# Next slot's tokens turned behind unit 31 into free halves of PSUM, and turns of one part side by side, in the expert stage of an encoder

## The reference, cut to what matters

```python
logits = (h @ router)                        # 8 experts
top_v, top_i = lax.top_k(logits, 2)
top_w = softmax(top_v)                       # gates
y = sum_e gates[:, e] * ((silu(h @ w1[e]) * (h @ w3[e])) @ w2[e])
# h: 256x1024, w1, w3: 8x1024x3584, w2: 8x3584x1024, float32
```

## Time and profile before

| | us |
|---|---|
| median of three runs | 1703.61 (1702.89 to 1704.52) |
| the profiled execution | 1703.97 |
| its span in the trace | 1702.1 |
| expert stage in it | about 700 to 1690 |
| PE busy | 1632.4 |
| DVE busy | 1249.7 |
| ACT busy | 1046.9 |

### The profile page before, as it was taken

How to read it: one execution, slowest core, us unless ns; L and a number is a source line. 1 busy time by engine, 2 the same in 40 slices (tenths; PEclk the granted TensorE clock), 3 DMA queues, 4 the chain that set the end, 5 groups by cost and what they waited for, 6 DMA issues and landing times.

```text
span 1702.1 us, 22766 instructions
## 1 busy us (share of the span) xinstructions
PE 1632.4 (96%) x8953; PEld 1403.5 (82%) x8953; DVE 1249.7 (73%) x916; ACT 1046.9 (62%) x926; POOL 101.7 (6%) x92
## 2 busy tenths in 40 slices
PE   5999999999999999899999999999999999999996
PEld 5899989999888998688787787787887887887885
DVE  4655575454565556798788887888887987987995
ACT  4364645343535463776676776776776776776774
POOL 1000001000000000110000000000000000000540
PEclk8999999999999999999999999999999999999999
DMA  7544459554654447999999999999999999999970
GB/s 240 193 143 148 149 192 341 184 189 151 227 176 143 148 149 285 352 372 419 348 374 369 363 369 347 368 369 350 377 377 335 387 377 336 387 377 336 406 312 25
DMA packets 162477, 488.97 MB, mean 287 GB/s; under 512 B 8176, under 2 KB 12368, under 8 KB 162416
## 3 DMA queue, kind: packets, MB, share of 16 engines
q1 hardware_dynamic: 154576, 459.17, 73.7%
q0 software_dynamic: 7552, 27.89, 4.3%
q10 hardware_dynamic: 288, 1.05, 0.2%
HBM read 471.82 MB, written 16.25 MB: 287 GB/s over the span
## 4 chain that ended last, share of the span: by engine, by line
PE 89%; ACT 4%; DVE 3%; issue 2%; DMA 2%; SPq 0%; DVEq 0%; ACTq 0%
PE big L1558 21%; PE big L1560 21%; PE big L1559 21%; PE small L1558 6%; PE small L1560 6%; PE small L1559 6%; PE small L1603 2%; ACT ehi L958 2%; DMA raw<-ffn_w 1%; DMA raw<-w_in 1%; ACT whi L756 1%; DVE elo L1378 0%; DVE wlo L1049 0%; PE small L1718 0%; PE small L1658 0%
## 5 line engine op out<-in xcount | busy, mean ns | idle before, releaser
L1378 DVE TENSOR_TENSOR elo<-eraw,ehi 128x2048 fp32r<-128x2048 f32 x336 | 772.7, 2318 | 137.2 <-ACT ehi L958 136.1
L958 ACT ACTIVATE ehi<-eraw 128x2048 fp32r<-128x2048 f32 x336 | 642.1, 1918 | 280.2 <-PE small L1560 147.2
L1049 DVE TENSOR_TENSOR wlo<-raw,whi 128x2048 fp32r<-128x2048 f32 (+2 forms) x104 | 229.9, 2218 | 202.6 <-ACT whi L756 202.6
L756 ACT ACTIVATE whi<-raw 128x2048 fp32r<-128x2048 f32 (+2 forms) x104 | 192.5, 1860 | 263.6 <-PE big L1560 187.9
L1558 PE MATMUL big<-ehi,hehi 128*128 128x512 f32 x896 | 352.0, 393 | 1.4 <-DVE helo L1423 1.4
L1560 PE MATMUL big<-ehi,helo 128*128 128x512 f32 x896 | 349.1, 390 | 0.0
L1559 PE MATMUL big<-elo,hehi 128*128 128x512 f32 x896 | 348.8, 389 | 0.0
L1558 PE MATMUL big<-hhi,whi 128*128 128x256 f32 x864 | 248.4, 288 | 9.4 <-DVE hlo L1069 8.6
L1560 PE MATMUL big<-hhi,wlo 128*128 128x256 f32 x864 | 246.0, 285 | 0.0
L1559 PE MATMUL big<-hlo,whi 128*128 128x256 f32 x864 | 245.9, 285 | 0.0
L1558 PEld LDWEIGHTS big<-ehi,hehi 128*128 128x128 f32 x896 | 168.3, 188 | 36.3 <-DVE helo L1423 1.6
(11 more groups left out here) (326 smaller groups left out, 1766.4 us busy)
## 6 DMA issues: line engine op xcount, KB each, us to landing
eraw<-moe_w SPq DMA_DIRECT2D x336, 1024.0 KB, 5.4
raw<-ffn_w SPq DMA_DIRECT2D x30, 1024.0 KB, 5.0
raw<-w_gate SPq DMA_DIRECT2D x24, 1024.0 KB, 5.0
raw<-w_in SPq DMA_DIRECT2D x20, 1024.0 KB, 5.2
raw<-w_branch SPq DMA_DIRECT2D x12, 1024.0 KB, 4.9
raw<-w_o SPq DMA_DIRECT2D x8, 1024.0 KB, 5.0
xs_all<-zeros POOLq DMA_DIRECT2D x12, 512.0 KB, 8.4
xn<-xs_all POOLq DMA_DIRECT2D x8, 512.0 KB, 6.0
```

The source lines that it names most:

```text
L756: act.activation(whi[u % HI][:, 0:kt, 0:cols], raw[u % RAW][:, 0:kt, 0:cols], ACT.Copy).then_inc(hi_ready, 1)
L958: act.activation(ehi[HI_OF[n]][:, :], eraw[n % RING][:, :], ACT.Copy).then_inc(ehi_ready, 1)
L1049: dve.tensor_tensor(wlo[u % RAW][:, 0:kt, 0:cols], raw[u % RAW][:, 0:kt, 0:cols], whi[u % HI][:, 0:kt, 0:cols].bitcast(F32), ALU.subtract) ...
L1378: dve.tensor_tensor(elo[n % RING][:, :], eraw[n % RING][:, :], ehi[HI_OF[n]][:, :].bitcast(F32), ALU.subtract).then_inc(elo_ready, 1)
```

## The change

`TURNS` changes so that the two parts of one pair are turned behind the same unit (10, 19, 31 instead of 9 and 10, 18 and 19, 30 and 31). The places where ScalarE and VectorE take them are now in a table of their own, `TAKEN`. The last part, still turned behind unit 37, is taken at unit 40 instead of 41. The next slot's tokens are turned in one block of eight behind unit 31, into the second halves of `big[0]` and `big[1]`, which pair 3 doesn't use, and taken at units 39 and 40 as before; ScalarE waits there for unit 35, the last that reads the old tokens. The turns of the last part no longer wait for a `helo` copy but for the copies of part 5.

```diff
--- before.py
+++ after.py
@@ -76,8 +76,13 @@
 
 
 
-TURNS = [9, 10, 18, 19, 30, 31, 37]
-GATHERS = [35, 36]
+
+TURNS = [10, 10, 19, 19, 31, 31, 37]
+TAKEN = [14, 14, 23, 23, 35, 35, 40]
+
+
+GATHERED = 31
+HE_TAKEN = [39, 40]
 HE = 2 * PAIRS - 1
 RING, EHI, EHI_WORK = 14, 4, 3
 EARLY = 3
@@ -733,9 +738,9 @@
         MIX_LOADS = 5
         BLOCK_COLS = ((0, P), (P, TOKENS))
 
-        def gather_bank(i):
-
-            return 3 - i
+        def gather_place(s, i):
+
+            return small[:, 3 - i, :] if isinstance(s, int) and s == 0 else big[i][:, 1, :]
 
         def flat2(ap):
             return ap.rearrange("p a n -> p (a n)")
@@ -960,7 +965,7 @@
             def gathered(s, i):
 
                 act.wait_ge(gather_done, 2 * s + i + 1)
-                act.activation(flat2(hehi[:, 4 * i:4 * i + 4, :]), small[:, gather_bank(i), :],
+                act.activation(flat2(hehi[:, 4 * i:4 * i + 4, :]), gather_place(s, i),
                                ACT.Copy).then_inc(hehi_ready, 1)
 
             def outputs(s, first=False):
@@ -993,14 +998,16 @@
                                 act.wait_ge(hid_turned, HE * s + 2 * p)
                             act.activation(hid[:, 0:pair_width(p)], flat2(big[0][0:SLOT, :, :])[:, 0:pair_width(p)],
                                            ACT.Silu).then_inc(sil_done, 1)
-                    if n - 4 in GATHERS:
-                        gathered(s + 1, GATHERS.index(n - 4))
-                    if n - 4 in TURNS:
-                        t = TURNS.index(n - 4)
-                        if first and t == HE - 1:
-
-                            act.wait_ge(scattered, 16 * 2 * NB)
-                        turned(s, t)
+                    for t in range(HE):
+                        if n == TAKEN[t]:
+                            if first and t == HE - 1:
+
+                                act.wait_ge(scattered, 16 * 2 * NB)
+                            turned(s, t)
+                    if n in HE_TAKEN:
+
+                        act.wait_ge(eunit_done, UNITS * s + unit_end(PAIRS - 1, 1) + 1)
+                        gathered(s + 1, HE_TAKEN.index(n))
 
 
             act.wait_ge(unit_done, NU)
@@ -1420,7 +1427,7 @@
             def gathered(s, i):
 
                 dve.wait_ge(hehi_ready, 2 * s + i + 1)
-                dve.tensor_tensor(flat2(helo[:, 4 * i:4 * i + 4, :]), small[:, gather_bank(i), :],
+                dve.tensor_tensor(flat2(helo[:, 4 * i:4 * i + 4, :]), gather_place(s, i),
                                   flat2(hehi[:, 4 * i:4 * i + 4, :]).bitcast(F32), ALU.subtract).then_inc(he_ready, 1)
 
             def gate_values():
@@ -1522,10 +1529,11 @@
                             cols = slice(0, pair_width(p))
                             dve.tensor_tensor(hid[:, cols], hid[:, cols], flat2(big[1][0:SLOT, :, :])[:, cols],
                                               ALU.mult).then_inc(act_done, 1)
-                    if n - 4 in GATHERS:
-                        gathered(s + 1, GATHERS.index(n - 4))
-                    if n - 4 in TURNS:
-                        turned(s, TURNS.index(n - 4))
+                    for t in range(HE):
+                        if n == TAKEN[t]:
+                            turned(s, t)
+                    if n in HE_TAKEN:
+                        gathered(s + 1, HE_TAKEN.index(n))
 
             slot(0, first=True)
             dve.wait_ge(routed, 1)
@@ -1876,7 +1884,7 @@
 
                 for k in range(4):
                     for b in range(NB):
-                        m = pe.matmul(small[:, gather_bank(i), SLOT * k:SLOT * k + SLOT], xn[:, b, (4 * i + k) * P:(4 * i + k + 1) * P],
+                        m = pe.matmul(gather_place(0, i)[:, SLOT * k:SLOT * k + SLOT], xn[:, b, (4 * i + k) * P:(4 * i + k + 1) * P],
                                       Gm[:, b, :], start=b == 0, stop=b == NB - 1)
                 m.then_inc(gather_done, 1)
 
@@ -1915,25 +1923,23 @@
                                 i = mm3(small[0:SLOT, half, :], ahi[:, t, :], alo[:, t, :], hi[:, k, cols], lo[:, k, cols],
                                         p == 0 and t == 0, n == UNITS - 1 and k == tiles - 1)
                     i.then_inc(eunit_done, 1)
-                    if n in TURNS:
-
-                        t = TURNS.index(n)
+                    for t in range(HE):
+                        if n != TURNS[t]:
+                            continue
                         pe.wait_ge(act_done, PAIRS * s + t // 2 + 1)
                         if t == HE - 1:
-                            pe.wait_ge(he_ready, 2 * s + 3)
+                            pe.wait_ge(alo_ready, HE * s + HE - 1)
                         for k in range(4):
                             c = 512 * (t % 2) + k * P
                             i = turn(small[:, turn_bank(t), SLOT * k:SLOT * k + SLOT], hid[:, c:c + P], SLOT)
                         i.then_inc(hid_turned, 1)
-                    if n in GATHERS:
-
-                        j = GATHERS.index(n)
-                        if j == 0:
-                            pe.wait_ge(xs_in, 16 * (s + 1))
-                            pe.wait_ge(alo_ready, HE * s + HE - 1)
-                        for k in range(4):
-                            i = turn(small[:, gather_bank(j), SLOT * k:SLOT * k + SLOT], xs[:, (4 * j + k) * P:(4 * j + k + 1) * P])
-                        i.then_inc(gather_done, 1)
+                    if n == GATHERED:
+
+                        pe.wait_ge(xs_in, 16 * (s + 1))
+                        for j in range(2):
+                            for k in range(4):
+                                i = turn(big[j][:, 1, SLOT * k:SLOT * k + SLOT], xs[:, (4 * j + k) * P:(4 * j + k + 1) * P])
+                            i.then_inc(gather_done, 1)
 
             busy(1)
             pe.wait_ge(xg_ready, NB)
```

## The result

| | us |
|---|---|
| before, median of four runs | 1703.25 (1701.88 to 1704.52) |
| changed kernel, median of four runs | 1661.89 (1660.92 to 1665.16) |
| ratio | 0.9761, 95% interval 0.9744 to 0.9778 |
| profiled execution before and after | 1703.97 and 1661.55 |
| span before and after | 1702.1 and 1659.8 |

The changed kernel is 2.4% faster. The forecast was 1663.4 us in a range of 1660 to 1672. Only one execution of each kernel has a trace. Of the changed kernel's other three, one took 1665.16 us at a mean granted clock of 0.994, where the rest had 0.997 to 0.999; it may have had drops of the clock, which no trace here shows. The lines of the changed kernel have moved: the matmuls are L1566 to L1568, a turn L1611, `helo` L1430, `last_lo` L1509, `last_hi` L980, `ehi` L963, `elo` L1385.

The account below looks back on a forecast made before the run. TensorE, busy 96% of the span, was taken as the bound, with two short waits a slot. Slots 35.2, turns 2.0 and clock 3.2 us made 40.4 off 1703.97; forecast 1663.4 us, range 1660 to 1672.

Parts of the forecast that it names:

- The wait before the turns of pair 3: TensorE after unit 37, waiting for the helo copy: saves 1.90 us a slot, plus 0.06 for the turns behind it.
- The wait before unit 40: TensorE after unit 39, waiting for VectorE's last_lo copy: goes whole, saving 2.44 us a slot.
- The starts added up at the slot's end: Units 36 to 41: unit 40 starts at 11.3 us; last_lo and elo of unit 41 each 0.7 us early.
- rivals 1 and 2: Slot's end: a small wait stays (13%, 1667 to 1675 us); the second wait stays whole (4%, 1683 us).
- Side by side: Turns in larger groups on TensorE: saves 0.25 us a slot, bounds a loss of 0.09 and a gain of 0.69.
- the row of eight: Eight turns on TensorE take 0.79 us, so a further turn costs 0.11 us; used to price sixteen.
- The clock: Lower granted clock behind the stalls: two drops of 1.6 us counted back, 3.2 us; bounds 0 and 3.2.
- The rule that a transpose does not count as busy: Sixteen turns behind unit 31 would be as good as idle; the rival with a drop each slot: 1676 us, 8%.
- Loads: DMA queues: a rival had weights unable to come faster, at 371 GB/s 121.5 us a slot, 1687 us, 6%.
- The sum: Whole kernel: slots 35.2, turns 2.0 and clock 3.2 us, together 40.4 us saved.

Follow-up runs that it names:

- e3: Kernel before with one edit, the last part taken at unit 40 instead of 41; 1678.81 us, ratio 0.9863.
- e4: Changed kernel with the turns of each pair apart again, behind units 9, 10, 18, 19, 30, 31; 1662.83 us.
- e2: Changed kernel with the take of the last part put back from unit 40 to unit 41; 1691.92 us.
- e7: Changed kernel with both token copies taken at unit 40, ahead of the last part's copies; 1665.98 us.
- e1: Kernel before with only the two parts of each pair turned behind one unit and taken together; 1701.90 us, ratio 0.9989.
- e5: Changed kernel with 48 more turns behind unit 31, 64 in a row; 1703.75 us in one execution.
- e9: Kernel of e2 with 19 turns written in the wait before unit 40, into a bank nobody reads; 1682.41 us.
- e6: Changed kernel with 11 more loads a slot, in all slots but the first, into a place nobody reads; 1661.64 us.
- e8: Kernel of e2 with four float32 matmuls of 512 columns written ahead of unit 40, into a bank nobody reads; 1689.93 us.

## Why the prediction was right

- **The wait before the turns of pair 3** (1.90 us, and 0.06): right. e3 against e4 gives 2.03 us a slot, of which 0.10 is the token turns standing in one row with part 5, so 1.93 for the 1.96 of the prediction.
- **The wait before unit 40** (2.44 us, saved whole): right, 2.60 in e3 and 2.56 in e2 against the changed kernel. The term was 0.14 too small: behind such a wait the next unit itself takes 2.86 us instead of 2.72, which I didn't price. Behind the first wait this costs nothing, since the turns that stand there slow the next unit by the same 0.14 without a wait.
- **The starts added up at the slot's end**: unit 40 at 11.3 us from unit 36 (measured 1049.74 - 1038.36 = 11.38), `last_lo` 0.7 us early (0.81), `elo` of unit 41 0.7 us early (0.73). e7 shows the second of these margins to be real; the third, the tightest, is untested. No wait is left at units 40, 41 or 0, so rivals 1 and 2 fall too.
- **Side by side** (0.25 us a slot, bounds -0.09 and 0.69): the row of eight was the right one to take. Sixteen turns took 1.67 us, 0.35 + 12 x 0.11 as worked out. e4 puts the pairs at 0.15, and 0.10 more is in the token turns' part, 0.25 together.
- **The clock** (3.2 us): right for this kernel, in the execution that has a trace. That the number was two before is partly luck: e1 keeps both waits and had four drops. e2 shows the size of the case that I did not have: six drops, 9.6 us, from one wait alone. The rule that a transpose does not count as busy in the way a matmul does (the Trainium skill, TensorE: Matmul & The Clock Gate, Part 4: PE-mode transpose) does not hold for the float32 turns here: 6.9 us of turns in e5 and 2.1 us of them in e9 kept the granted clock at 1.00, in the very place where 2.3 us of idleness lost it. The page's figures are for bf16, which no run here has, and whether turns can raise the clock from the lower level is not shown either.
- **Loads**: a DMA share of 1.01 at 367 GB/s was no limit; e6 moved 419. The figure of about 358 GB/s on the HBM side (the Trainium skill, DMA: Bandwidth & Descriptors, Where 436 GB/s comes from), half of what a stack gives two cores, is passed by both kernels on this single busy core (366 and 371 GB/s).
- **The sum** (40.4 us by the trace, 42.4 measured): 1.1 of the difference is the slow unit behind each of the eight second waits, 0.8 lies ahead of the expert stage and has no cause shown. That the total came so near has some luck in it: the stage ahead happened to be shorter, and the medians differ by 41.4, not 42.4.

## What to carry to other kernels

When an engine that is busy 96% of the time has a short wait in each turn of a loop, look for whose buffer or place in the program that wait stands behind, add up the starts of the three engines at that place from their own rows, and move the copy ahead of work that isn't needed yet. Read the margin that is left in the same way; it is the next wait. From these runs, a wait of some 2 us on TensorE costs its length, plus 0.14 us where matmuls stand right behind it, plus the chance of a clock drop of 1.6 us.

## What the runs showed of the hardware

- The granted clock fell behind a wait of 2.3 us before unit 40 in 2 of 8 slots (before), 3 of 8 (e1) and 6 of 8 (e2), for about 1.6 us each time, and behind none of the eight waits of 1.7 us where they stood alone (e3), though once behind such a first wait in e1 (1.9 us, in slot 0). A kernel with one wait less (e2) so had more drops than the one with both. Filling the wait took all drops away (e8, e9), so idleness is what they need; why some slots have one and others not is left open.
- A float32 turn of 128x128 costs 0.109 us in a long row (e5), and 0.11 from four to eight and from eight to sixteen.
- Behind a wait or a group of turns the next 12 matmuls take some 2.86 us instead of 2.72 (unit 40 in e7, unit 38 in the changed kernel).
- A float32 matmul of 512 columns stands as two in the trace (e8: 4 written, 8 shown) and takes 0.86 us, against 0.227 for one of the rounded ones.
- The queues of one core held 419 GB/s over a whole slot with TensorE at full pace (e6).
